# Second attention's mask moved from matmuls into the scan, with a new order of splits, root table and spread at the state space's end

## The reference, cut to what matters

```python
# the state space layer's end: 4 groups of 512 channels, each normalised by itself
y = y.reshape(b, s, M_D_INNER) * jax.nn.silu(z)
yg = y.reshape(b, s, M_GROUPS, M_D_INNER // M_GROUPS)
yg = yg * lax.rsqrt(jnp.mean(yg * yg, axis=-1, keepdims=True) + EPS)
y = yg.reshape(b, s, M_D_INNER) * norm_g
return y @ out_w

# stick-breaking attention, for each block i of 128 queries (lo:hi)
z = jnp.einsum('bthd,bshd->bhts', q[:, lo:hi], k[:, :hi]) * scale
mask = (lo + jnp.arange(128))[:, None] > jnp.arange(hi)[None, :]
log_keep = jnp.where(mask, log_sigmoid(-z), 0.0)
after = cumsum(log_keep, axis=3, reverse=True) - log_keep
a = exp(jnp.where(mask, log_sigmoid(z) + after, -inf))
out = jnp.einsum('bhts,bshd->bthd', a, v[:, :hi])
```

## Time and profile before

| | |
|---|---|
| median of 3 runs | 1415.16 us (1412.99 to 1416.69) |
| the profiled execution | 1413.45 us, span 1411.7 us |
| mean granted clock of TensorE | 0.975 |
| TensorE busy | 1347.8 us, 95% of the span |
| VectorE busy | 820.0 us, 58% |
| ScalarE busy | 588.4 us, 42% |
| GpSimd busy | 407.1 us, 29% |
| state space's output panels | about 985 to 1088 us |
| norm, keys, values, first queries | about 1091 to 1197 us |
| second attention's 32 blocks | about 1197 to 1362 us |

### The profile page before, as it was taken

One profiled execution on the slowest core, in us unless ns is written; L12 is line 12 of the kernel. 1 busy time (PEld: TensorE's weight loads), 2 busy tenths in 40 slices (PEclk: granted clock), 3 DMA queues, 4 the chain that ended last, 5 costly groups with the idle time before them and its releaser, 6 DMA issues. The chain is left out here.

```text
span 1411.7 us, 19533 instructions
## 1 busy us (share of the span) xinstructions
PE 1347.8 (95%) x7904; PEld 1073.8 (76%) x7904; DVE 820.0 (58%) x965; ACT 588.4 (42%) x849; POOL 407.1 (29%) x191
## 2 busy tenths in 40 slices
PE   5999999889999999999999999999898999999996
PEld 3778867578888888887788876767786899777775
DVE  2789974576555544334757656778723822566544
ACT  4323656332222232113444456787522422455441
POOL 0000000149978877998100000000000050232310
PEclk9999999889999999999799999999999999999998
DMA  9434071124454464554222243334222432111121
GB/s 384 148 141 149 31 263 66 60 90 178 178 200 179 160 233 179 198 188 149 93 91 89 92 132 92 113 119 143 90 79 89 161 121 90 60 60 34 57 90 60
DMA packets 41350, 181.12 MB, mean 128 GB/s; under 512 B 3392, under 2 KB 20160, under 8 KB 21312
## 3 DMA queue, kind: packets, MB, share of 16 engines
q1 hardware_dynamic: 40128, 171.73, 33.8%
q10 hardware_dynamic: 1152, 8.39, 1.7%
HBM read 173.75 MB, written 6.36 MB: 128 GB/s over the span
## 5 line engine op out<-in xcount | busy, mean ns | idle before, releaser
L193 DVE TENSOR_TENSOR wlo<-raw,whi 128x2048 fp32r<-128x2048 f32 x95 | 257.9, 2714 | 174.6 <-ACT whi L189 172.0
L200 POOL TENSOR_TENSOR ada_raw<-ada_raw,cs 128x2048 f32<-128x2048 f32 x36 | 144.8, 4024 | 499.5 <-DVE h2lo L451 451.0
L271 PE MATMUL ps<-hhi,whi 128*128 128x512 f32 x640 | 252.0, 394 | 2.4 <-PEq L563 0.8
L271 PE MATMUL ps<-hhi,wlo 128*128 128x512 f32 x640 | 249.4, 390 | 0.0
L271 PE MATMUL ps<-hlo,whi 128*128 128x512 f32 x640 | 249.1, 389 | 0.0
L189 ACT ACTIVATE whi<-raw 128x2048 fp32r<-128x2048 f32 x95 | 181.6, 1911 | 144.4 <-PE ps L1312 91.3
L209 POOL TENSOR_TENSOR ada_raw<-ada_raw 128x1024 f32<-128x1024 f32 x72 | 168.1, 2334 | 5.6
L271 PEld LDWEIGHTS ps<-hhi,whi 128*128 128x128 f32 x640 | 120.2, 188 | 28.7 <-issue 2.4
L271 PEld LDWEIGHTS ps<-hhi,wlo 128*128 128x128 f32 x640 | 120.1, 188 | 25.8
L271 PEld LDWEIGHTS ps<-hlo,whi 128*128 128x128 f32 x640 | 120.3, 188 | 24.2
L2050 POOL TENSOR_TENSOR x<-x,rest 128x256 f32<-128x256 f32 (+3 forms) x32 | 49.0, 1532 | 160.2 <-DVE rest L2349 160.2
(11 more groups left out here) (374 smaller groups left out, 2774.0 us busy)
## 6 DMA issues: line engine op xcount, KB each, us to landing
raw<-panels SPq DMA_DIRECT2D x87, 1024.0 KB, 4.9
ada_raw<-ada SPq DMA_DIRECT2D x48, 1024.0 KB, 6.7
first<-ada SPq DMA_DIRECT2D x8, 1024.0 KB, 21.1
bc<-ac_rows SPq DMA_DIRECT2D x32, 256.0 KB, 3.6
raw<-panels ACTq DMA_DIRECT2D x8, 1024.0 KB, 5.0
x_kept<-x SPq DMA_DIRECT2D x2, 2048.0 KB, 9.6
x<-x_kept SPq DMA_DIRECT2D x2, 2048.0 KB, 7.7
x<-x_in SPq DMA_DIRECT2D x1, 2048.0 KB, 9.9
```

What stands on the lines that cost most here:

```text
L193: e.tensor_tensor(wlo[:, c % 2, :, :], raw[:, c % 2, :, :], whi[:, c % 2, :, :].bitcast(F32), ALU.subtract).then_inc(lo_split, 1)
L200: e.tensor_tensor(ada_raw[:, c % 2, :, :], ada_raw[:, c % 2, :, :], cs[:, which, :].unsqueeze(2).to_broadcast([P, KT, 256]), ALU.mult).the ...
L271: mm = e.matmul(ps[:, 2 * (qc % 2) + b, :], w[:, c % 2, 2 * k + b, :], src[part][:, k, :], **flags)
```

## The change

- The attention's mask: the two matmuls at L2080 go. The third pass of the logits closes the sums and carries the semaphore. The last column of `rest` is 0 and the scan starts at 0. Its second operand is a new tensor `own`, 128 x 512: zeros, but the identity in its last 128 columns, read backwards like `rest`. For keys behind the query the running value is thus 0; at the query's own key it becomes 1; from there it is the product of `rest` as before. `own` takes the place in memory of `exact`, which nothing uses any more by then. It is set where `zero` was set before.
- ScalarE's order at the state space's end: the one-column Sqrt and the split of panel `cm + 2` come before the squares of group 3 and the high parts of group 2.
- VectorE's order there: the low part of `cm + 2` before `norm_lo(2)`.
- TensorE's: `group_spread(3)` at (2, 2) in place of (2, 1).
- The two coefficient tables of the next block's norms are made at the end of `norm_lo(3)`.

```diff
-        exact = sbuf(ctx, "exact", [P, 4, P], F32R)
+        exact, own = shared_sbuf(ctx, ("exact", [P, 4, P], F32R), [("own", [P, S], F32)])
...
+        def norm_coefs(dve, gain, sc, slot, k0=0, k1=KT):
+            dve.scalar_tensor_tensor(out=coef[:, slot, k0:k1], in0=m(sc)[:, k0:k1], scalar=1.0, in1=gain[:, k0:k1],
+                                     op0=ALU.add, op1=ALU.mult).then_inc(nsem["coef_ready"], 1)
...
-                                if (k, j) == (2, 1):
+                                if (k, j) == (2, 2):
                                     group_spread(3)
...
+                        act.activation(warm[:, 5:6], ones[:, 0:1], ACT.Sqrt)
+                        split_hi(act, cm + 2, 0)
                         group_squares(3)
                         hi_part(act, 2)
-                        split_hi(act, cm + 2, 0)
                         group_std(3)
                         split_hi(act, cm + 3, 0)
                         hi_part(act, 3)
-                        act.activation(warm[:, 5:6], ones[:, 0:1], ACT.Sqrt)
...
+                        split_lo(dve, cm + 2, 0)
                         norm_lo(dve, 2)
-                        split_lo(dve, cm + 2, 0)
                         group_rs(dve, 3)
                         split_lo(dve, cm + 3, 0)
                         norm_lo(dve, 3)
+                        norm_coefs(dve, v("kv_norm"), "kvsc", 1)
+                        norm_coefs(dve, v("norm2", KT, KT), "ssc", 2)
...
-                                pe.matmul(ps[:, 2 + e, 0:nw], q[r0:r0 + HD, t % QS, qb * P:nk],
-                                          k[r0:r0 + HD, t, 0:nw], start=u == 0, stop=False, skip_group_check=True)
-                        for e in range(2):
-                            mm = pe.matmul(ps[:, 2 + e, qb * P:nk], ident_r, exact[:, CST["neg_from"], :],
-                                           start=False, stop=True, skip_group_check=True)
+                                mm = pe.matmul(ps[:, 2 + e, 0:nw], q[r0:r0 + HD, t % QS, qb * P:nk],
+                                               k[r0:r0 + HD, t, 0:nw], start=u == 0, stop=u == 2, skip_group_check=True)
...
-                    pre3["coefs"](dve)
-                    pre4["coefs"](dve)
                     pre3["dve"](dve)
                     split_lo(dve, c0 + 1, 0)
-                    dve.memset(zero[:], 0.0).then_inc(B["zero"], 1)
-                    dve.memset(rest[:, :, :, S:S + 1], 1.0).then_inc(B["zero"], 1)
+                    dve.memset(own[:, 0:S - P], 0.0).then_inc(B["own"], 1)
+                    dve.tensor_copy(own[:, S - P:S], ident).then_inc(B["own"], 1)
+                    dve.memset(rest[:, :, :, S:S + 1], 0.0).then_inc(B["own"], 1)
...
-                                scan = dve.tensor_tensor_scan(turned, turned, zero[:, 0:1].to_broadcast([P, nk]),
-                                                              1.0, ALU.mult, ALU.add)
+                                scan = dve.tensor_tensor_scan(turned, turned, own[:, S - nk:S][:, ::-1], 0.0,
+                                                              ALU.mult, ALU.add)
```

More of the change, by code:

```diff
@@ L442, in coefs @@
             def coefs(dve, k0=0, k1=KT):
-                dve.scalar_tensor_tensor(out=coef[:, slot, k0:k1], in0=m(sc)[:, k0:k1], scalar=1.0, in1=gain[:, k0:k1],
-                                         op0=ALU.add, op1=ALU.mult).then_inc(N["coef_ready"], 1)
+                norm_coefs(dve, gain, sc, slot, k0, k1)
             def on_dve(dve, k0=0, k1=KT):
@@ L1992, in build @@
             rest = sbuf(seg, "rest", [P, 2, 2, S + 1])
-            zero = sbuf(seg, "zero", [P, 1])
             h0 = rest[:, 0, :, 0:S]
@@ L1999, in build @@
             fsq = v2[:].rearrange("p a (b s) -> p (a b) s", b=2)
-            B = {k: sem("b_" + k) for k in ("zero", "z_done", "sig", "keep", "rest", "am", "t_done", "amt",
+            B = {k: sem("b_" + k) for k in ("own", "z_done", "sig", "keep", "rest", "am", "t_done", "amt",
                                             "pv_done", "og", "ohi", "olo", "half", "khi", "qhi", "qfree", "zsig",
@@ L2311, in _ @@
                             read_mod(dve, NADA - 2, NADA)
-                    dve.wait_ge(B["zero"], 2)
+                    dve.wait_ge(B["own"], 3)
                     def turn_half(mh):
```

## The result

| | before | after |
|---|---|---|
| median | 1414.08 us (4 runs) | 1402.03 us (4 runs, 1400.56 to 1405.93) |
| ratio, 95% interval | | 0.991 [0.9881, 0.9939] |
| ratio in a second set of runs (the changed kernel once more, below) | | 0.9905 [0.9891, 0.9918] |
| the profiled execution, and its span | 1413.45, 1411.7 us | 1405.93, 1404.1 us |
| output panels: second spread to the last sum of the norm behind | 88.11 us | 82.50 us |

The two stages that the change touches give 5.61 and 6.84 us; both lengths are differences of starts, the first from the spread at 999.22 (the one at (1, 1)) to the last sum at 1087.33 (after: 1003.34 to 1085.84), the second from 1197.84 to 1361.06 in the chain (after: 1197.58 to 1353.96).

A forecast was written before the change was run, and what follows sets the result against it. TensorE was taken to bound the attention stage, with a hole at the state space's end. 6.8 + 5.5 + 0.2 = 12.5 us off 1413.45 gives 1401.0; the forecast was 1402.0, range 1395.5 to 1408.

The forecast's parts named there:

- The mask: Attention on TensorE: each removed pair of mask matmuls frees 0.22 us, one block's share lost, 6.8 us gained.
- The order: State space's end: earlier split and low half remove TensorE's hole (4.0) and low-clock matmuls (1.5), 5.5 us gained.
- The table load: ScalarE at the state space's end: switching to Sqrt costs 1.28 us by the trace, 2.66 by the skill page.
- The coefficient tables: Two coefficient instructions behind the block's boundary move to where VectorE later idles: 0.2 us gained.
- The scan: Attention on VectorE: a full-row second operand adds 0.03 us to each of 64 scans, nothing on the path.
- Rival D: Attention: a real second operand stretches scans beside GpSimd's product, 2.6 times if all; time 1435; chance 0.03.
- The constants: Table built once on VectorE: a 384-column memset and 128-column copy, each bounded by 0.49 us, cost nothing.
- Rival B: State space's end: the hole stays in part, gain there only 1 to 2 us, time 1406; chance 0.14.

The follow-up runs named there:

- the changed kernel once more: The changed kernel run again, unedited, beside the other experiments for a narrower interval: 1400.98 us, ratio 0.9905 [0.9891, 0.9918].
- a real row alone: Kernel before, mask matmuls kept; scans of up to 384 columns read a real row of zeros instead of the broadcast zero: attention 163.21 us.
- the doubled load: Changed kernel with a further scan of up to 384 columns, output unused, before each scan on VectorE: attention 167.47 us, 11.1 longer.
- the pair doubled: Kernel before with each block's pair of mask matmuls issued twice: attention 169.97 us, 6.75 longer.

## Why the prediction was right, point by point

- **The mask, 6.8 us.** Measured 6.84, 6.82 alone. Taking starts of weight loads, not the chain's durations, was the choice that mattered: the chain's 0.37 would have given 11.5. The mechanism is right; that the sum fits to the hundredth is in part luck, because two of its terms are off against each other. The prediction read one wait of TensorE in the stage and took one pair for lost, 31 x 0.22. There are two, and both grew, as the waits above show. The wait for `v`, right before the first projection, swallows block 0's pair; that leaves the 31 pairs that stand behind it. A pair is worth 0.23 by the turns, 7.2 us for 31, and block 29's wait takes back 0.4 of it, nearly two pairs and not one: 6.8.
- **The order, 5.5 us.** Measured 5.61. With 4.12 us taken off, the steps read: split done at 1004.3 (forecast 1004.3), low half 1006.6 (1006.6), first low part 1008.7 (1008.7), third panel begun 1009.64 (1009.64), reciprocal 1012.8 (1013.1), spread 1015.3 (1015.3). The third panel took 12.1 us (12.2), from its start and the start of the fourth, which lies as far ahead of the last sum as before. The delay of 0.1 us by the squares is real: undoing it gave 0.1 back.
- **The table load.** Load and Sqrt started 1.29 us apart, as in the earlier trace rows; the drain of 1.38 us that the Trainium skill ("ScalarE: Activation LUTs", section "What ACT_TABLE_LOAD costs") adds did not show. The split began 1.40 us behind the load's start, so the row was the right choice. That the load was worth moving the prediction didn't claim; it isn't.
- **The coefficient tables, 0.2 us.** 0.21.
- **The scan, nothing.** Its shortest is 392 ns still, and a real row alone changed nothing. Rival D's condition isn't met; that a full VectorE decides is shown by the doubled load. Rival D's sum took the 2.6 of the earlier trace rows for a factor on every scan. It isn't one: what a scan loses is the time that it lies beside the product. Its threshold of 2.1 holds for the turn of 20.6; for the 19.7 that it names the factor is 2.0.
- **The constants, nothing.** The memset of 384 columns took 0.38 and the copy 0.16 us, under the bound of 0.49 each, and VectorE still idled 1.99 us behind them.
- **Rival B** did not come: the first low part led by 1.0 us, the forecast's 0.8 and a little.
- The time came out at 1402.0 as forecast; to the tenth that is luck, since single executions of either kernel differ by about 4 us and more. That the sum of 12.5 meets 12.65 in the traces rests on the stages' mechanisms and not on chance, except for the two terms of the mask named above.

## What to carry to other kernels

Price an instruction in a saturated TensorE queue by the starts of weight loads on both sides of it, and check what it absorbs of its neighbour's start-up; the duration that a chain books for it can be over half too much (here 0.37 for 0.22). Where an engine hands over a panel that another must split and a third must wait for, the low half's place in VectorE's order has to move with the high half's; the high half's move alone gained 0.5 of 5.6 us here. A hole in front of dense matmuls costs more than its length, so remove it before shortening the matmuls. Look for what is behind a freed stretch, too: both waits of TensorE that stood there grew, by 0.4 us each. And where a scan shares its time with a GpSimd product, count the product's remaining time, not a factor.

## What was not expected

- **The second cost of a hole.** A hole of 3.4 to 3.9 us cost the panels 5.15 to 5.61 us in every kernel that had one, and none of those without one fell from full clock there.
- **The norm behind the panels.** It has its own waits, of 1.15, 1.47 and 1.97 us, and among them the clock falls, in every one of the fourteen traces. In four (the first profile of the whole change, the mask alone, the order alone, the pair doubled) it fell up to 0.8 us before the spread and stood low for about 10 us; in the other ten it fell behind the spread's start and stood low for about 7. Both kinds are there with and without each part of the change, so no part of it alone decides which comes. Windows there (clock in the third column from the end), the kernel before and then the changed one:

```profile
1087.50:1090.00 2.50, 1.03 (x14) 0.77 (x7) 0.95 (x1) 2.17 (x2) 0.00 (x0) 0.96 0.00 0
1090.00:1092.50 2.50, 0.80 (x4) 0.51 (x3) 1.37 (x4) 0.38 (x1) 0.00 (x0) 0.50 0.30 46
1092.50:1095.00 2.50, 2.02 (x5) 1.66 (x6) 2.33 (x4) 1.56 (x3) 0.00 (x0) 0.50 0.87 360
1095.00:1097.50 2.50, 2.50 (x9) 1.96 (x8) 2.43 (x5) 1.05 (x3) 0.00 (x0) 0.67 0.99 419
```

```profile
1087.50:1090.00 2.50, 2.07 (x8) 1.78 (x8) 0.19 (x1) 1.00 (x1) 0.00 (x0) 0.50 0.00 0
1090.00:1092.50 2.50, 0.71 (x2) 0.65 (x3) 2.20 (x4) 1.38 (x2) 0.00 (x0) 0.50 0.57 138
1092.50:1095.00 2.50, 2.50 (x8) 1.94 (x7) 2.46 (x4) 1.03 (x2) 0.00 (x0) 0.50 1.02 429
1095.00:1097.50 2.50, 2.50 (x8) 1.96 (x7) 2.43 (x5) 1.14 (x2) 0.00 (x0) 0.51 0.64 272
```

Here the changed kernel has the low clock about 3 us longer. The same 48 matmuls took from 12.86 to 14.02 us, and the spread before them 1.16 to 2.08. From the last sum to the end of the 48 this makes 18.4 to 19.9 us; the coefficient tables are 0.2 of it. The larger scatter lies before the second spread, 8.4 us between the earliest and the latest; what makes it there stays open.
